# Making the rounded weights of a GLA projection on ScalarE instead of GpSimd

## The reference

```python
def odd_mixer(h, gla_s, w_in, w_gate2, b_gate, norm_w, w_out):
    proj = (h @ w_in).astype(jnp.float32)
    q, k, v, r, glr = jnp.split(proj, ODD_SPLITS, axis=-1)
    gate_logit = glr @ w_gate2 + b_gate
    log_a = (jax.nn.log_sigmoid(gate_logit) / GLA_TAU).reshape(B, T, GLA_HEADS, GLA_DK)
    o, s_new = gla_chunked(q, k, v, log_a, gla_s.astype(jnp.float32))   # chunks of 64 in the reference
    o = head_rms(o) * norm_w
    mix = (jax.nn.silu(r) * o.reshape(B, T, GLA_VALUE)).astype(h.dtype) @ w_out
    return mix, s_new
```

## Time and profile before

| | |
|---|---|
| Profiled execution | 2751.67 us, span 2749.8 us |
| Median of three executions | 2751.99 us (2748.38 to 2754.41) |
| TensorE matmul busy | 2614.2 us (95%) |
| VectorE busy | 1352.9 us (49%) |
| ScalarE busy | 623.6 us (23%) |
| GpSimd busy | 854.3 us (31%) |
| Mean granted TensorE clock | 0.963 of full speed |

### The profile page before, as it was taken

One profiled execution on the slowest core, in us unless ns is written; L12 is line 12 of the kernel. 1 busy time (PEld: TensorE's weight loads), 2 busy tenths in 40 slices (PEclk: granted clock), 3 DMA queues, 4 the chain that ended last, 5 costly groups with the idle time before them and its releaser, 6 DMA issues. The chain is left out here.

```text
span 2749.8 us, 38422 instructions
## 1 busy us (share of the span) xinstructions
PE 2614.2 (95%) x15196; PEld 2510.2 (91%) x15196; DVE 1352.9 (49%) x2101; ACT 623.6 (23%) x1048; POOL 854.3 (31%) x383
## 2 busy tenths in 40 slices
PE   7999879999999999999789999998999999999998
PEld 7898639999999999999778898888999999999997
DVE  6763354553443344336585655645553443343345
ACT  3610142320011011003532423333220111011013
POOL 3342102433333333334211211113333333333350
PEclk9999969999999999999898989889999999999999
DMA  3011002111111111111210111102111111111111
GB/s 134 31 56 39 31 25 106 47 39 47 47 47 39 47 46 46 39 47 55 80 39 33 47 45 35 56 31 98 47 47 41 45 47 47 41 45 46 47 54 66
DMA packets 39231, 137.78 MB, mean 50 GB/s; under 512 B 5952, under 2 KB 9664, under 8 KB 37792
## 3 DMA queue, kind: packets, MB, share of 16 engines
q1 hardware_dynamic: 32192, 104.55, 11.4%
q10 hardware_dynamic: 6880, 30.87, 2.9%
HBM read 120.52 MB, written 14.88 MB: 49 GB/s over the span
## 5 line engine op out<-in xcount | busy, mean ns | idle before, releaser
L524 PE MATMUL PS<-RA,WH 128*128 128x384 f32 (+1 forms) x4608 | 1132.2, 329 | 23.4 <-DVE RA L1254 12.4
L524 PE MATMUL PS<-RB,WH 128*128 128x384 f32 (+1 forms) x4272 | 1073.4, 335 | 4.2 <-DVE X L1310 4.2
L494 POOL TENSOR_TENSOR WH<-WR,ZERO 128x1024 fp32r<-128x1024 f32 x185 | 354.7, 1917 | 1815.4 <-PE PS L524 1806.2
L524 PEld LDWEIGHTS PS<-RA,WH 128*128 128x128 f32 x4608 | 816.7, 189 | 34.9 <-issue 18.3
L524 PEld LDWEIGHTS PS<-RB,WH 128*128 128x128 f32 x4272 | 774.6, 193 | 12.3 <-DVE X L1310 5.2
L524 PE MATMUL PS<-RA,WL 128*128 128x384 f32 (+1 forms) x2304 | 754.7, 328 | 0.0
L524 PE MATMUL PS<-RB,WL 128*128 128x384 f32 (+1 forms) x2136 | 708.7, 332 | 0.0
L497 POOL TENSOR_TENSOR WL<-WR,WH 128x1024 fp32r<-128x1024 f32 x185 | 482.2, 2607 | 14.5
L524 PEld LDWEIGHTS PS<-RA,WL 128*128 128x128 f32 x2304 | 434.3, 189 | 0.0
L524 PEld LDWEIGHTS PS<-RB,WL 128*128 128x128 f32 x2136 | 411.3, 193 | 0.0
L1310 DVE TENSOR_TENSOR X<-PS,X 128x384 f32<-128x384 f32 x360 | 189.6, 534 | 440.6 <-PE PS L524 440.6
(11 more groups left out here) (207 smaller groups left out, 1684.5 us busy)
## 6 DMA issues: line engine op xcount, KB each, us to landing
WR<-ws SPq DMA_DIRECT2D x189, 512.0 KB, 3.2
X<-xT ACTq DMA_DIRECT2D x8, 544.0 KB, 7.9
EB<-xT ACTq DMA_DIRECT2D x8, 544.0 KB, 8.8
x_spill<-X ACTq DMA_DIRECT2D x1, 4352.0 KB, 11.9
EB<-x_spill ACTq DMA_DIRECT2D x8, 544.0 KB, 7.0
GA<-st_gla ACTq DMA_DIRECT2D x4, 1024.0 KB, 5.5
glas_o<-GA ACTq DMA_DIRECT2D x4, 1024.0 KB, 3.9
yT<-X SPq DMA_DIRECT2D x16, 192.0 KB, 1.9
```

What stands on the lines that cost most here:

```text
L494: nc.gpsimd.tensor_tensor(WH[:, slot, :], WR[:, slot, :], ZERO[:, 0:1].to_broadcast([P, 1024]), ALU.add).then_inc(w_high, 1)
L524: return nc.tensor.matmul(out, lhsT, rhs, start=start, stop=stop, skip_group_check=True)
```

## The change

For steps 94 to 117 (`ACT_FIRST` to `ACT_END`, 24 steps, which are units 2 to 24 and the first step of the output projection behind them) GpSimd no longer makes the high part. ScalarE does, with a Copy from WR to WH, at the item `("S", u, 2)` of the unit that used the slot before, behind that unit's Silu where it has one. GpSimd's loop is cut in two around 24 written-out low parts, which wait for the high part through `w_high`.

```diff
+ACT_FIRST, ACT_END = B_ODD_IN + 2, B_ODD_OUT + 1
@@ GpSimd
-            with pool.Fori(1, (N_STEPS - 4) // 2) as i:
+            def low_part(n):
+                slot = n % 2
+                pool.wait_ge(w_loaded[slot], 16 * (n // 2) + 16)
+                pool.wait_ge(gemm_done, 6 * n - 6)
+                pool.wait_ge(w_high, n + 1)
+                nc.gpsimd.tensor_tensor(WL[:, slot, :], WR[:, slot, :], WH[:, slot, :].bitcast(F32),
+                                        ALU.subtract).then_inc(w_split, 1)
+            with pool.Fori(1, ACT_FIRST // 2) as i:
+                for slot in range(2):
+                    parts(2 * i + slot, i, slot, False)
+            for n in range(ACT_FIRST, ACT_END):
+                low_part(n)
+            with pool.Fori(ACT_END // 2, (N_STEPS - 4) // 2) as i:
                 for slot in range(2):
                     parts(2 * i + slot, i, slot, False)
@@ ScalarE, at the end of the item "S"
+                    n = B_ODD_IN + u + 2
+                    if g == 2 and n < ACT_END:
+                        act.wait_ge(w_loaded[n % 2], 16 * (n // 2) + 16)
+                        act.wait_ge(gemm_done, 6 * n - 6)
+                        A(WH[:, n % 2, :], WR[:, n % 2, :], ACT.Copy).then_inc(w_high, 1)
```

More of the change, by code:

```diff
@@ L61 @@
 MS_BANK = (6, 7, 6)
+ACT_FIRST, ACT_END = B_ODD_IN + 2, B_ODD_OUT + 1
+assert ACT_FIRST % 2 == 0 and ACT_END % 2 == 0
 def second(n):
```

## The result

| | before | changed |
|---|---|---|
| Median | 2747.41 us (20 runs, 2742.03 to 2754.41) | 2756.13 us (20 runs, 2750.07 to 2762.88) |
| Ratio to before | | 1.003, 95% interval 1.0023 to 1.0036 |
| Profiled execution | 2751.67 us | 2755.13 us |
| Mean granted clock of the profiled execution | 0.963 | 0.962 |

The change makes the kernel 8.7 us slower. The profiled pair differs by 3.5 us only: the profiled execution of before took 4.3 us more than the median of 20.

The account below looks back on a forecast made before the run. TensorE, busy for 95% of the span, was taken as the bound, leaving only its short waits and clock to change. Losses of 8.0 + 0.6 less gains of 5.8 made +2.8 us on the profiled 2751.67: 2754.5 us, range 2747 to 2761.

Parts of the forecast that it names:

- Within 0.2%: Forecast outcome that the change cannot be told from no change (0.2% is 5.5 us): chance 0.53, against 0.34 for slower.
- The Copy at 1.03 and the hand-over of 0.1: ScalarE's 1024-column Copy takes 1.03 us; GpSimd's low part begins 0.1 us after it.
- The losses at five places, 8.0 us: Steps 102, 104, 108, 110, 114: Copy delays squares, low part blocks VectorE's add, TensorE waits 1.6 us more each.
- Steps 97 and 98, 0.6 us: Late Copy at step 97 makes its low part block VectorE; TensorE's restart moves by 0.6 us, between nothing and 2.
- The gains, 5.8 us: Shorter TensorE waits for VectorE at steps 95, 96, 99, 100, 101, 105, 107, 111 and 113, together 5.8 us.
- Steps 105 and 111: Line 1588 and the work behind it get through before the low part; TensorE's 1.03 us wait shortens by about 0.6 each.
- What was to stay: Steps 106, 112, 115 and 116: low part starts 0.2 later, ends where it did; the wait of 2.77 stays, gain 0.
- with no TensorE wait near them: The remaining eight of the 24 steps, where the change was to gain or cost 0.
- The clock: Rival: the clock falls behind two or three of the five new waits, giving 2757.5 to 2759.0 us; chance 0.26.
- The sign that the prediction had named for being wrong: Line 870 starting at once at the five places, waits of steps 99 and 101 staying, or half-clock stretches changing by over two.
- The add goes ahead: Rival: at the five places VectorE's add runs before GpSimd's low part, the 8.0 us fall away, 2746.5 us; chance 0.16.
- nothing changes: Rival: TensorE's score matmuls take up the squares' delay and the gains shift waits only, 2751.7 us; chance 0.14.

Follow-up runs that it names:

- the two sets: The changed kernel's first runs and a repeat of it unchanged for a second profile, each against before: ratios 1.003 and 1.0023.
- Five only: Kernel before with only the high parts of steps 102, 104, 108, 110 and 114 made on ScalarE: ratio 1.0049 to before, median 11.0 us more.
- squares first: Changed kernel with the Copy behind the norm's squares at steps 102, 104, 108, 110 and 114: ratio 0.9966 to before, median 11.1 us less.
- add first: Changed kernel, but GpSimd's low part waits for VectorE's norm add at steps 102, 104, 108, 110 and 114: ratio 0.9962 to before.
- three only: Kernel before with only the high parts of steps 101, 107 and 113 made on ScalarE: ratio 0.9986 to before, median 5.2 us less.
- GpSimd waits: Kernel before, no Copy on ScalarE; GpSimd waits with both parts for VectorE's add at eleven norm steps: ratio 0.9961, median 10.4 us less.

## Why the prediction came out as it did

The forecast of 2754.5 us stands 1.6 under the 2756.1 measured, but partly by two errors that cancel: the change costs 8.7 and 6.9 us in the two sets, not 2.8, and the base of 2751.67 was 4.3 too high. "Within 0.2%" was given the larger chance, and the change is slower by 0.30% and 0.23%.

- **The bound, and the high parts worth nothing as work:** right. In the GLA stage TensorE waits for GpSimd in neither profile, so GpSimd's 48 us less bought nothing as work.
- **The Copy at 1.03 and the hand-over of 0.1:** 1.05 us. At step 102 the low part starts 1.22 behind the Copy's start, 0.16 behind its end.
- **The losses at five places, 8.0 us:** right in place and mechanism, and nearly in size: 3 x 1.79 + 2 x (1.85 - 0.15) = 8.8 us. "Five only" and "squares first" show the order, "add first" the lock.
- **Steps 97 and 98, 0.6 us:** nothing. The wait of 2.92 is now two:

```profile
1372.43 0.33 PE L803 MATMUL PS<-CST,GA 128*128 128x128 f32 x1 [1.08 <-DVE GA L1710]
...
1376.39 1.11 PE L822 MATMUL PS<-GA 128*128 128x64 f32 x4 [1.89 <-DVE GA L1727]
```

  1.08 + 1.89 = 2.97.
- **The gains, 5.8 us:** 4.4. Steps 99 and 100 gave 0.7 each (0.8 forecast), 96 gave 1.2 (1.0), 95 0.3 (0.5), 101, 107 and 113 0.4 each (0.5). Steps 105 and 111 gave 0.1 each, not 0.6: the lock did go (VectorE's line 1610 takes 0.55 where 1588 took 1.85), but VectorE then stands idle 2.14 us for TensorE's next columns (line 1292 reads them from PSUM), so line 1727, which TensorE waits for, comes when these do:

```profile
1551.81 0.55 DVE L1610 TENSOR_TENSOR X<-X,OD 128x384 f32<-128x384 f32 x1
...
1556.93 0.56 DVE L1292 TENSOR_TENSOR OD<-PS,RS 128x384 f32<-128x384 f32 x1 [2.14 <-PE PS L541]
```

  The prediction took a lock ahead of a wait for its cause, without following what released the last instruction before it.
- **What was to stay:** the waits of 2.77 us at steps 106 and 112 and of 1.45 at 115 and 116 stayed. The steps "with no TensorE wait near them" are four (94, 103, 109 and 117), not eight; the sum had them at nothing, so it is not touched.
- **The waits' sum** is then 8.8 + 0.05 - 4.4 = +4.5 us, where 2.8 was forecast. Outside the norm waits the gains are 0.34 (step 95), 1.21 (96), 1.23 (101, 107 and 113) and 0.18 (105 and 111), together 3.0.
- **The clock** is the step that failed. The forecast had it at nothing; it stood there as a rival with 0.26, priced at 1.5 us per stretch, and "three only" bears that price out roughly: its 5.2 us less 1.2 of waits are 1.3 us for each of three stretches. Two things were wrong. The chance was too low: the prediction saw one 1.21 us wait followed by a half-clock stretch and still took the fall as the exception. And it was weighed on one side only: it asked what the longer waits would bring and not what the shortened ones would take away, where three stretches went. In the profiled pair both nearly cancel (four stretches came and three went at the places named), and the pair differs by 3.5 us; over the runs 10.9 us more at half clock, three stretches' worth, are left against the change, about 4.6 us (2.3 in the second set). The sign that the prediction had named for being wrong, a change by more than two stretches, shows in the runs and not in the profiled pair. "The add goes ahead" and "nothing changes" did not happen.
- What stays open: why the half clock of one kernel differs by 5.6 us between two sets of runs (208.8 and 203.2; the scatter of single runs may be all of it), why "GpSimd waits" has more half clock than before with shorter waits, and what decides whether a given wait brings a fall: behind step 101's wait it came in 13 of 15 cases at 1.2 us or more and in none of 21 at 0.8; behind the new waits of 1.8 in 11 of 15. No wait of a length between was tried.

## What to carry to other kernels

Before moving work to an idle engine, ask what the moved instruction waits for and what is queued behind it: a Copy of 1 us that stood 3.6 us at a semaphore turned a gain of 11 us into a loss of 9, and putting it behind that work at five steps turned it back. Where GpSimd and VectorE both work in SBUF, let the long GpSimd instruction wait for the short VectorE one that TensorE needs; this wait at eleven places was worth 10.4 us, about as much as moving the high parts with the squares first (11.1), and both together were worth 20.6. Judge changes to waits of about a microsecond by the granted clock over many runs, not by one profiled pair.

## What the hardware showed that was not expected

- A wait shortened from 1.2 to 0.8 us was worth some four times its 0.4 us, since 3.4 us at half clock behind it went as well (three places: 5.2 us by the medians; the interval of the ratio, 0.9977 to 0.9996, is 1.1 to 6.3 us).
- The lock works both ways: where VectorE has its own run of two-input work, GpSimd's low part of 2.4 us took 3.72.
- ScalarE's Copy of the weights takes 1.04 to 1.06 us in all 24 steps; the one of step 97 took 1.04 while VectorE ran adds with two inputs in SBUF beside it. Unlike GpSimd's instructions, it held VectorE up nowhere that was looked at: those adds took their usual 0.35 and 0.55.
